# The half swap of the rotation by DMA copies, the values' meta rows in two products with a joint stationary, and the input in one array

## What is computed

```python
h = concatenate([meta, x])                 # 16 + 512 rows of 1024
xn = rmsnorm(h, ln1_w)
dq, dk, dv, gq, gk, gv, gr, zf, zb = split(xn @ w_in)
# dq, dk: 4 heads x 2 x 64, the first 16 of each 64 are rotated by position:
x1, x2 = xr[..., :8], xr[..., 8:16]
rot = concatenate([x1 * cos - x2 * sin, x2 * cos + x1 * sin])
```

## Time and profile before

| what | us |
|---|---|
| median of three runs | 2368.0 (2366.3 to 2369.91) |
| span of the profiled execution | 2362.3 |
| TensorE busy | 2298.3 (97% of the span) |
| VectorE busy | 1691.2 (72%) |
| ScalarE busy | 1113.7 (47%) |
| GpSimd busy | 579.9 (25%) |
| DMA | 470.79 MB, mean 199 GB/s |

### The profile page before, as it was taken

The page is one execution under the profiler, slowest core; times in us unless marked ns, Lnnn a source line. Parts: engine busy times, 40 slices in busy tenths (PEclk is TensorE's granted clock), DMA queues, the critical chain, the costliest instruction groups (busy, mean ns, idle before and its releaser), DMA issues.

```text
span 2362.3 us, 40246 instructions
## 1 busy us (share of the span) xinstructions
PE 2298.3 (97%) x14434; PEld 1368.9 (58%) x14434; DVE 1691.2 (72%) x3071; ACT 1113.7 (47%) x1728; POOL 579.9 (25%) x442
## 2 busy tenths in 40 slices
PE   7999899999999999999999999999999999999998
PEld 4446767655555566665555555564454465445885
DVE  5327766588899979977888888878453448777236
ACT  4266443766666678863333333342622234333134
POOL 0001002567888642224322222204000010000011
PEclk9999999999999999999999999999999999999999
DMA  5200022588899669999999999933233323333322
GB/s 183 81 27 1 1 72 90 167 279 308 310 323 327 223 206 355 355 356 356 381 361 359 367 360 357 365 133 107 89 109 106 98 73 124 107 101 99 109 75 72
DMA packets 165903, 470.79 MB, mean 199 GB/s; under 512 B 17744, under 2 KB 72784, under 8 KB 165008
## 3 DMA queue, kind: packets, MB, share of 16 engines
q1 hardware_dynamic: 110336, 289.48, 36.9%
q0 software_dynamic: 36864, 134.23, 15.3%
q10 hardware_dynamic: 18576, 45.36, 4.9%
HBM read 421.56 MB, written 47.45 MB: 199 GB/s over the span
## 4 chain that ended last, share of the span: by engine, by line
PE 74%; DVE 17%; ACT 3%; issue 2%; DMA 1%; DVEq 1%; POOL 1%; SPq 0%; POOLq 0%; ACTq 0%
PE psum L689 22%; PE psum L691 22%; PE psum L690 22%; DVE arena L2496 4%; DVE arena L663 1%; DVEq L2421 1%; DMA arena<-in_urows,arena 1%; ACT arena L650 1%; PE psum L1311 1%; PE psum L1156 1%; PE psum L1312 1%; PE psum L1034 1%; DVE arena L2262 1%; DVE arena L2434 1%; DVE arena L2432 1%
## 5 line engine op out<-in xcount | busy, mean ns | idle before, releaser
L689 PE MATMUL psum<-arena 128*128 128x384 f16 (+5 forms) x3984 | 1311.7, 331 | 18.9 <-POOL arena L669 4.6
L690 PE MATMUL psum<-arena 128*128 128x384 f16 (+5 forms) x3984 | 1314.9, 330 | 0.0
L691 PE MATMUL psum<-arena 128*128 128x384 f16 (+5 forms) x3984 | 1308.5, 330 | 0.0
L689 PEld LDWEIGHTS psum<-arena 128*128 128x128 f16 (+1 forms) x3984 | 386.4, 97 | 319.9 <-issue 29.3
L691 PEld LDWEIGHTS psum<-arena 128*128 128x128 f16 (+1 forms) x3984 | 385.3, 97 | 290.0 <-issue 1.3
L690 PEld LDWEIGHTS psum<-arena 128*128 128x128 f16 (+1 forms) x3984 | 385.3, 97 | 278.3 <-issue 2.6
L663 DVE SCALAR_TENSOR_TENSOR arena<-arena 128x1024 f16<-128x1024 f32 x216 | 265.0, 1231 | 256.4 <-ACT arena L650 255.5
L650 ACT ACTIVATE arena<-arena 128x1024 f16<-128x1024 f32 x216 | 226.2, 1051 | 228.8 <-PE psum L691 217.4
L1940 ACT ACTIVATE arena<-arena 128x1024 f16<-128x1024 f32 x128 | 135.3, 1057 | 297.7 <-PE psum L691 281.4
L669 POOL TENSOR_TENSOR arena<-arena 128x1024 f16<-128x1024 f32 x104 | 230.0, 2211 | 79.5 <-ACT arena L658 78.4
L2886 POOL DMA_INDIRECT arena<-in_v,arena x128 | 137.4, 1073 | 351.9 <-DVE arena L2507 319.6
(11 more groups left out here) (274 smaller groups left out, 2238.8 us busy)
## 6 DMA issues: line engine op xcount, KB each, us to landing
arena<-in_w SPq DMA_DIRECT2D x320, 512.0 KB
arena<-in_v SPq DMA_DIRECT2D x128, 512.0 KB
early_activations<-arena ACTq DMA_DIRECT2D x124, 192.0 KB
arena<-early_activations SPq DMA_DIRECT2D x124, 192.0 KB
gate_matrix<-arena ACTq DMA_DIRECT2D x5, 4096.0 KB, 18.0
arena<-gate_matrix SPq DMA_DIRECT2D x32, 640.0 KB
arena<-in_xT SPq DMA_DIRECT2D x4, 512.0 KB, 6.1
arena<-in_urows,arena POOLq DMA_INDIRECT x128
```

The costliest lines, as they stand in the source:

```text
L689: nc.tensor.matmul(ps, a_h, b_h, start=first, stop=False)
L690: nc.tensor.matmul(ps, a_h, b_l, start=False, stop=False)
L691: return nc.tensor.matmul(ps, a_l, b_h, start=False, stop=last)
```

## The change

Six edits, all at the first block's start except the last:

1. The rows of the rotation are swapped by DMA. SP issues for each of the eight query and key chunks, once it is evicted, four copies of 8 rows inside the on-chip memory into `swapped`, a double buffer that GpSimd has cleared; VectorE rotates from it two chunks later. The products `rope_swap` and the constant `perm` are gone.
2. The values' meta rows: GpSimd places the high and the low half of the 16 meta tokens side by side in one 128 wide stationary (`xm`, high at columns 0 to 15, low at 32 to 47, the rest zero). Two products, with the high and the low half of the weights, give the four combinations; ScalarE takes rows 32 to 47 to `mrow`, VectorE adds rows 0 to 15 (`meta_values`).
3. The input is one array with the meta columns at each row's end, so each quarter of `X` is one DMA of whole rows. `ident` comes behind it, counted with `vec`.
4. `pick` is set by GpSimd instead of being loaded.
5. VectorE's operations on `vec` stand behind the additions of the squares.
6. The table for the root is loaded ahead of the squares, in `ln1` and in `mixn`.

```diff
-            sp.dma_start(X[:, :, T:TM], io["metaT"]).then_inc(meta_in, 16)
             for i in range(XL):
                 c = slice(i * KC // XL, (i + 1) * KC // XL)
-                sp.dma_start(X[:, c, 0:T], io["xT"][:, c, :]).then_inc(x_in[i], 16)
-                if i == 0:
-                    sp.dma_start(pick, io["pick"]).then_inc(picks_in, 16)
-                    sp.dma_start(ident, io["ident"]).then_inc(picks_in, 16)
+                sp.dma_start(X[:, c, :].rearrange("p a b -> p (a b)"),
+                             io["xT"][:, c, :].rearrange("p a b -> p (a b)")).then_inc(x_in[i], 16)
+            sp.dma_start(ident, io["ident"]).then_inc(vecs_in, 16)
             sp.dma_start(vec, io["vec"]).then_inc(vecs_in, 16)
...
-            slabs(SLOTS, N_WO)
+            def swap_rows(n):
+
+                b = n % 2
+                sp.wait_ge(rope_in, n + 1)
+                if n == 0:
+                    sp.wait_ge(pool_step, SWAP_CLEAR)
+                wait(sp, rope_done, n - 1)
+                src = q[:, n, :] if n < HEADS else k[:, n - HEADS, :]
+                for c in range(2):
+                    x1, x2 = (slice(DH * c + i * ROPE, DH * c + (i + 1) * ROPE) for i in range(2))
+                    for to, of in ((x1, x2), (x2, x1)):
+                        sp.dma_start(swapped[to, b, 0:T if n < HEADS else TM], src[of]).then_inc(swap_in[b], 16)
+
+            slabs(SLOTS, 2 * SLOTS)
+            for n in range(N_Q, N_V):
+                swap_rows(n)
+                sp.wait_ge(low_cut, n + 2 * SLOTS + 1 - SLOTS)
+                sp.dma_start(wraw[:, slot(n), :], io["w"][n + 2 * SLOTS]).then_inc(slab_in[slot(n)], 16)
+            slabs(N_V + 2 * SLOTS, N_WO)
...
-                if n >= 1:
-                    rope_swap(n - 1)
-            rope_swap(N_V - 1)
-
+
+            pe.wait_ge(consts_in, 176)
+            pe.wait_ge(pool_step, META_CUT)
...
-                            last = parts(psum[0:P if t < TT else M, b * 512:(b + 1) * 512],
-                                         xh[:, 2 * g + c, cols], xl[:, 2 * g + c, cols], w_h, w_l,
-                                         g == 0 and c == 0, g == 3 and c == 1)
+                            if t < TT:
+                                cols = slice(t * P, (t + 1) * P)
+                                last = parts(bank(b), xh[:, 2 * g + c, cols], xl[:, 2 * g + c, cols], w_h, w_l,
+                                             g == 0 and c == 0, g == 3 and c == 1)
+                            else:
+                                both = xm[:, 2 * g + c, :]
+                                nc.tensor.matmul(bank(b), both, w_h, start=g == 0 and c == 0, stop=False)
+                                last = nc.tensor.matmul(bank(b), both, w_l, start=False, stop=g == 3 and c == 1)
...
-                if c == KC - 2 and self.i < len(NORMS) - 1:
-                    roots_table(self.i)
...
-            act.wait_ge(pool_step, 1)
+            act.wait_ge(pool_step, EPS_SET)
             n1 = Norm("ln1", 6)
-            act.wait_ge(meta_in, 16)
+            roots_table(n1.i)
...
+            act.wait_ge(rope_done, N_V)
...
             n4 = Norm("mixn", 7, sums=0)
+            roots_table(n4.i)
...
-            dve.wait_ge(vecs_in, 16)
+            n1 = Norm("ln1", 6)
+            n1.add_squares(dve, nc.vector)
+            dve.wait_ge(vecs_in, 32)
...
+                dst, cols = (q[:, n, :], T) if n < HEADS else (k[:, n - HEADS, :], TM)
+                other = swapped[:, n % 2, 0:cols]
+                dve.wait_ge(swap_in[n % 2], 64 * (n // 2 + 1))
+                nc.vector.tensor_tensor(other, other, ropes[:, 0:cols], ALU.mult)
+                dchain.link(nc.vector.tensor_tensor(dst, dst, ropec[:, 0:cols], ALU.mult))
+                nc.vector.tensor_tensor(dst, dst, other, ALU.add).then_inc(rope_done, 1)
 
             for n in range(N_Q, N_V):
                 cuts.upto(n + 3)
-                if n >= 1:
-                    rope(n - 1)
+                if n >= 2:
+                    rope(n - 2)
+            rope(N_V - 2)
             rope(N_V - 1)
...
+            for part, dst in enumerate((dv, gv)):
+                cuts.upto(N_V + 4 * part + 7)
+                dve.wait_ge(values_out, 5 * (part + 1))
+                nc.vector.scalar_tensor_tensor(out=dst[0:M, TT, :], in0=bank(value_bank(part, TT))[0:M], scalar=ISW,
+                                               in1=mrow[0:M, part, :], op0=ALU.mult,
+                                               op1=ALU.add).then_inc(meta_values, 1)
...
+            nc.gpsimd.memset(pick, 0.0).then_inc(pool_step, 1)
+            pool.wait_ge(pool_step, EPS_SET + 1)
+            nc.gpsimd.memset(pick[:, TT:TT + 1], 1.0).then_inc(pool_step, 1)
             nc.gpsimd.memset(z32[0:DH], 1.0).then_inc(pool_step, 1)
+            nc.gpsimd.memset(swapped.rearrange("p a b -> p (a b)"), 0.0).then_inc(pool_step, 1)
+            nc.gpsimd.memset(xm.rearrange("p a b -> p (a b)"), 0.0).then_inc(pool_step, 1)
+            n1 = Norm("ln1", 6)
+            pool.wait_ge(pool_step, META_CLEAR)
+            for x, at, cut in ((xh, 0, xh_done), (xl, 32, xl_done)):
+                pool.wait_ge(cut, n1.chunks + KC)
+                nc.gpsimd.tensor_copy(xm[:, :, at:at + M], x[:, :, T:TM]).then_inc(pool_step, 1)
```

More of the change, by code:

```diff
@@ L158, in build @@
         iota = base.take(P)
-        perm = base.take(P)
         pick = base.take(TT + 5)
@@ L842, in _ @@
                 sp.dma_start(wraw[:, s, :], io["w"][s]).then_inc(slab_in[s], 16)
[L843 removed]
+            for dst, name in ((ones, "ones"), (iota, "iota"), (masks, "masks"), (ropec, "ropec"),
                               (ropes, "ropes"), (icnt, "icnt"), (io16, "io16"), (w2[0:DH], "w2"), (wz, "wz"),
@@ L924, in _ @@
                              stop=True).then_inc(lam_step, 1)
+            pe.wait_ge(vecs_in, 32)
             n1.spread(pe)
-            def rope_swap(n):
-                if n == 0:
-                    pe.wait_ge(consts_in, 192)
-                pe.wait_ge(rope_in, n + 1)
-                src = q[:, n, :] if n < HEADS else k[:, n - HEADS, 0:T]
-                if n >= 1:
-                    pe.wait_ge(rope_mul, n)
-                last = nc.tensor.matmul(bank(6), perm, src, start=True, stop=True)
-                if n >= HEADS:
-                    last = nc.tensor.matmul(bank(7, M), perm, k[:, n - HEADS, T:TM], start=True, stop=True)
-                last.then_inc(rope_out, 1)
             for n in range(N_Q, N_V):
@@ L1623, in _ @@
                 for t in range(5):
-                    rows = P if t < TT else M
                     b = value_bank(part, t)
-                    nc.scalar.activation(dst[0:rows, t, :], psum[0:rows, b * 512:(b + 1) * 512], ACT.Copy,
-                                         scale=ISW).then_inc(values_out, 1)
+                    if t < TT:
+                        nc.scalar.activation(dst[:, t, :], bank(b), ACT.Copy, scale=ISW).then_inc(values_out, 1)
+                    else:
+                        nc.scalar.activation(mrow[0:M, part, :], bank(b)[32:32 + M], ACT.Copy,
+                                             scale=ISW).then_inc(values_out, 1)
             act.wait_ge(gate_mm, 1)
-            act.wait_ge(pool_step, 2)
+            act.wait_ge(pool_step, PICK_SET + 1)
             nc.scalar.activation(z32[0:M, 0:T], psum[0:M, 2 * 512:3 * 512], ACT.Copy, scale=ISW).then_inc(z_out, 1)
@@ L3025, in layout @@
     out = {
-        "xT": fm(f["x"][0]), "metaT": fm(f["meta_tokens"]), "vec": np.concatenate(vecs, 1), "w": w,
+        "xT": np.concatenate([fm(f["x"][0]), fm(f["meta_tokens"])], 2), "vec": np.concatenate(vecs, 1), "w": w,
         "w2": w2, "wz": wz.reshape(KC, P, DH).transpose(1, 0, 2).reshape(P, KC * DH),
```

57 lines of the change are left out of this document (18 added, 39 removed).

## The result

The changed kernel runs in 2344.7 us (median of four runs, 2344.05 to 2351.57; the kernel before, with one more run beside them, 2367.15). The ratio is 0.9910, 95% interval 0.9895 to 0.9925. In the profiled executions the span went from 2362.3 to 2342.3 us, 20.0 less, where 18.5 was forecast. One of the five timings of a later variant (early values and fillers), 2849 us at a mean clock of 0.78, belongs to a slower state of the chip and is left out.

A forecast was written before the change was run, and what follows sets the result against it. TensorE's line was taken to bound the kernel. Gains of 3.3 + 8.4 + 6.6 + 0.2 = 18.5 us took the median from 2368.0 to 2349.5 us, range 2344.5 to 2357.

The forecast's parts named there:

- Front: 0 to 23 us: earlier input and reordered work bring the first normalisation's reciprocal forward by 3.3 us, ends 1.9 and 4.1.
- All three paths: At the first reciprocal: ScalarE ready at 14.1 us, TensorE at 14.0, VectorE's two slab cuts at 14.5; the last wins.
- TensorE path (14.0): Before the first reciprocal: input at 4.9, square 0.65, sums 5.97, grouped sums 2.11, root 0.34, ending at 14.0 us.
- Swaps: Queries and keys: swap products leave TensorE's line, 1.22 + 4.84 + 2.34 = 8.4 us, after a new 0.93 us wait.
- Copies: Queries and keys: four copies a chunk on SP, at most 2.5 us of issue, stay covered and cost zero.
- the slower rival: Queries and keys: SP holds for each copy's whole landing instead of its issue; about 2381 us, chance 0.03.
- a sign of error: Queries and keys: VectorE waiting on the copies by more than 2 us would show the prediction wrong.
- Values: 78 to 133 us: 16 narrow meta-row groups fall from 0.84 to 0.43 us each, 6.6 us gained, lower end 3.4.
- half of two terms: Narrow group's extra time stays (3.4 us gained) and input comes only 1.9 us earlier; 2354.1 us, chance 0.12.
- Table in `mixn`: At 1578 us: loading the root's table earlier, in ScalarE's idle time, gains 0.2 us, not 1.28.
- Clock: At the pair's first products and the sums near 1580 us: clock losses can move some 1.5 us either way.
- From span to median: Whole kernel: the median lies 5.7 us above the profiled span, so a span of 2343.8 becomes 2349.5 us.

The follow-up runs named there:

- early values and fillers: Changed kernel with TensorE's wait for the last key eviction moved to the values' fourth group, plus unread products in TensorE's idle time in `ln1` and `mixn`: 2344.7 us, ratio 0.9911.
- the run with 48 columns: Changed kernel with the joint stationary of the meta rows cut from 128 to 48 columns, same two products a group: 2350.4 us, ratio 0.9928.

## Why the prediction was right, point by point

The terms at the place where they act were right to 0.6 us each. That the median of 2344.7 lies inside the range, 0.2 above its lower end, is luck: 3.3 us of the distance to the forecast come from which execution was traced (last point below), and the later median of 2347.3 lies well inside.

- **Front, 3.3 forecast, 3.93 measured.** All three paths that were to meet were there, and the last was VectorE's cut of two slabs, as said. What was too cautious is the landing: the last quarter was there at 8.86, not at 9.4, and the second slab's high cut started at 11.91. The prediction's TensorE path (14.0) was right to 0.1 by another sum: 5.65 + 7.92 + root. That the first table load no longer stands between input and square was in its arithmetic (4.9 + 0.65) but not named as a gain, and the expectation for the run with the loads back then forgot it.
- **Swaps, 8.4 forecast, 8.24 measured**, against the kernel before and again against the run with the products back. The 0.16 lie between the eviction's end and TensorE's start, 65.54 to 65.79, where 0.08 was put.
- **Copies, zero forecast, zero measured.** An issue took 0.63 in the median, which had been put as the most, once 1.00, four of them 2.6 to 3.0, and they landed within 3.5 to 4.0 of their issue. The point from which the slower rival decides was put at some 2 us of SP per copy of 8 rows; 1.2 (eight copies) costs nothing, 2.4 (sixteen) 36 us. The estimate of 8.2 us that followed from the Trainium skill (DMA: Bandwidth & Descriptors, the anatomy of one DMA) for four copies served one after the other isn't met; the section fits its fixed time on DMAs that GpSimd issues, and these are SP's. Chunk 7's were issued from 65.56 and VectorE had them at 69.97. Where the prediction failed is a detail beside the path: VectorE did wait more than 2 us, 4.07 at the last chunk, which it had named as a sign of error. There no key chunk and no cut stands between the copies and the rotation, and the cover is the time until slab 11 is wanted.
- **Values, 6.6 forecast, 18.57 - 12.20 = 6.37 measured**. A half slab lost 0.42 where 0.41 was reckoned; what is missing is mostly the new wait of 0.24 between the two parts, which the sum didn't have. The reason given for the extra 0.19 of a group, the change of the stationary's width, is shown by the run with 48 columns; the rival that saw the extra time in bank or position (*half of two terms*) falls.
- **Table in `mixn`, 0.2 forecast, 0.55 measured.** The step that failed is reading the cover off 0.18 us of waiting. The clock had fallen within the sums before that wait (2.05 for 16, where 1.85 were measured at full clock), and slow work hides a late input: at full clock the wait is 0.39. The rest of what was won there is the clock's.
- **Clock, +-1.5 forecast.** In the first trace of the changed kernel it cost 3.1 at 176 and gave back 1.9 at 780, some 1.3 in `mixn` and 0.8 at the end. The falls at 176 and at 780 (762 in the changed kernel) are each there in one trace of the changed kernel and absent in the other, and in `mixn` the fall came before or behind the last sums in traces of either kernel; so these aren't put down to the change. The 0.8 at the end wasn't looked into.
- **From span to median.** The forecast took over a distance of 5.7 us between the median and the profiled span. In all runs with a span printed beside the time, that distance is 1.7 to 2.8. So the traced execution of the kernel before took, as an estimate, about 2364 us, 3.9 below the median of 2368.0, and the changed kernel's 0.65 below its own. Those 3.3 us and the 1.5 by which the spans' difference beat the forecast are the 4.8 between 2349.5 and 2344.7. Against the later median of 2347.3 it is 2.2.

## What to carry to other kernels

Count SP's microseconds per step of the bounding engine and not the landing of a copy: with steps of 5.2 to 5.8 us the small copies inside the on-chip memory cost nothing while SP needed up to 5.5 a step, and 36 us when it needed 10.2. Keep every stationary in a row of products at the same width, padded with zeros if need be: a change cost about 0.1 us on the way in and on the way out, for 512 columns of fp16 at full clock. And when an edit is worth 1 to 5 us in a kernel whose runs differ by as much, compare the time of one instruction right behind it, beside the count of slow products, and not the end.

## What was not expected

- A weight load is not done ahead when the width changes: 0.31 us from product to product where it is 0.2155 otherwise, for 48 columns as for 16.
- The clock falls at the same few places, but not in each execution, behind waits of TensorE of as little as 1.05 us. With products that nobody reads, four ahead of the first sum and five in the 2.4 us of idle time ahead of the pair, the pair started with 0 and 4 slow products instead of 7 to 14; in `mixn` the same did nothing. The Trainium skill (TensorE: Matmul & The Clock Gate, What's actually happening) says that the number of slow products at a start varies from run to run; the traces agree, with 7, 10, 11, 12, 13 and 14.
- Two things differ from one execution to the next and are each of the size of the spread between single runs: waits of 2.8 to 3.0 us behind the gathers of the experts' rows, and falls of the clock behind waits of TensorE, which cost 1.5 us (at 250), 1.9 (at 780) and 3.1 (at 176) where it was read. How much of the spread they make wasn't measured, since only one execution of each run has a trace.
